# Expert sum and residual as diagonal matmuls in PSUM, last norm from PSUM, and SyncE waiting for the scatters itself

## The chip, the cores and the metric

The kernel runs on one core of a Trainium2 chip. The metric is the device time of one launch in microseconds (us), as the median of several runs. The core has five engines that run programs of their own and meet at semaphores: TensorE (PE, with its weight loads as PEld), VectorE (DVE), ScalarE (ACT), GpSimd (POOL) and SyncE (SP), which here only issues transfers. A smaller number is better.

## What is computed

One transformer layer on 512 tokens of width 1024: attention and a state space layer, a first layer norm, and then a mixture of 64 experts of which each token uses two. The change lies in the last two lines, where the two expert rows of a token are weighted and summed, the scaled residual is added, and the result is normalised.

```python
def layer_norm(x, g, b):
    mu = mean(x); var = mean((x - mu)**2)
    return (x - mu) * rsqrt(var + LN_EPS) * g + b

x = layer_norm(DN_ALPHA * x + mixed @ w_out, ln1_g, ln1_b)   # 512 x 1024, float32
# router: for every token two experts e0, e1 and two weights w0, w1
# y0 = expert_e0(x), y1 = expert_e1(x)       (silu(x @ w_gate) * (x @ w_up)) @ w_down
y_m = w0 * y0 + w1 * y1
x = layer_norm(DN_ALPHA * x + y_m, ln2_g, ln2_b)             # the output
```

## The kernel before

**Stages.** Projections, attention and the state space layer run first. Then comes the first norm, and after it the router. From the router's choices VectorE builds tables: which expert each block of 64 tokens uses (`ids`), which tokens are in it (`gidx`), and where its rows are written (`sidx`). The names `idf` and `ids` stand for one row of numbers on one partition; `ids[MAXB]` holds `extra`, how many blocks there are beyond the first eight (`FORCED`). After `ids` is written (semaphore `s_idr`), VectorE goes on in the same program to the tables that free the first gather (`s_slot`, `s_idx`).

**Expert stage.** Per block SP loads the expert's weights (3 MB, six slots), POOL gathers the tokens from DRAM (`x1_dram`), PE turns them, multiplies (`gate_up` at L725, `down` at L745), ACT copies the result out of PSUM (L952), and POOL scatters it by an indirect transfer to a DRAM buffer `ye_scratch` (L1554). Each engine has its own copy of the loop: 6 rounds of 12 steps, each step inside an `If` that is skipped once the step's number reaches `extra`. In this case 62 blocks run, so 54 of the 72 steps of the loop are taken and the last 18 are skipped.

**Tail.** The text below calls what follows the last block the tail. POOL, behind its loop, waits until all scatters (`s_sct`) and gathers have landed and raises `s_moe`. SP waits for it (L378) and issues four loads, one for each tile of 128 tokens: both expert rows of a token, 1 MB each, into `yt`. VectorE then does `combine(t)`: row 0 times its weight plus the residual `x1t` (L1461; ACT has multiplied the residual by `ALPHA` during the router, at L938), row 1 times its weight added (L1462), and the sums of the norm (`norm_stats`, L1283 to L1286). ACT takes the square root (L970) and, after two small VectorE operations (`scales2`, L1467 and L1468), forms the normalised tile (L974). VectorE multiplies by the gain (L1478), POOL adds the offset (L1584), and SP writes the tile out (L381). The order on VectorE is written by hand: the sum of tile j, the scales of tile j-1, the gain of tile j-2.

Matmuls are in float32; 512 columns fill one PSUM bank, `ps[0]` to `ps[7]`. `s_ye` says that ACT has emptied a result bank.

## Time and profile before

| | us |
|---|---|
| median of 3 runs | 1080.71 |
| lowest, highest | 1080.68, 1081.19 |
| the profiled execution's own time | 1079.19 |
| its span in the trace | 1077.4 |

All times of the trace are counted from the start of the span. A row of the chain of waits or of the timeline gives the start, the length and the instruction; "L1462" is line 1462 of the kernel. "Idle before" is what the engine waited for ahead of an instruction. PEclk is the granted clock of TensorE: 1.00 is 2.4 GHz and 0.50 is 1.2 GHz. In this trace each float32 matmul that is not a transpose shows as two records.

### The profile page before, as it was taken

The numbers are of one execution on the slowest core, as the hardware profiler recorded it, in microseconds if no ns is written. First come the engines' busy times: TensorE is split into PE (matmuls) and PEld (weight loads), VectorE is DVE, ScalarE is ACT, GpSimd is POOL, SyncE is SP. The second block draws the span as 40 slices with busy tenths as digits, with TensorE's granted clock in tenths as the row PEclk, the third lists the DMA queues.
The fourth block names the chain that finished last, engine by engine and source line by source line (L and its number), as shares of the span: only waits on it lengthen the run. The fifth ranks groups of instructions, "written<-read, shape, count | busy, mean of one in ns | idle before, by whom it ended". The sixth has DMA issues, their size and how long they took to land.

```text
span 1077.4 us, 14172 instructions
## 1 busy us (share of the span) xinstructions
PE 883.6 (82%) x4862; PEld 492.9 (46%) x4862; DVE 312.7 (29%) x769; ACT 182.1 (17%) x400; POOL 175.6 (16%) x271
## 2 busy tenths in 40 slices
PE   7999887989999999998458888888888777788800
PEld 3446774544444444345435555555544344444400
DVE  5970744760111111144431111111111111111145
ACT  1223136661000100000201111111111010110111
POOL 2010002440000000000012222222222222222203
PEclk9999978999999999999569999999999999999955
DMA  8332903018222110532429999999999999999241
GB/s 285 72 87 69 116 22 142 1 69 351 113 100 99 69 69 0 203 133 112 161 78 411 420 421 420 421 421 422 422 421 422 421 424 424 424 424 408 91 158 78
DMA packets 43307, 253.36 MB, mean 235 GB/s; under 512 B 15304, under 2 KB 15832, under 8 KB 25956
## 3 DMA queue, kind: packets, MB, share of 16 engines
q1 hardware_dynamic: 32596, 242.58, 57.2%
q0 software_dynamic: 10528, 9.72, 3.5%
q8 instruction: 24, 0.39, 0.2%
q10 hardware_dynamic: 144, 0.55, 0.1%
q14 instruction: 15, 0.11, 0.0%
HBM read 256.27 MB, written 21.04 MB: 257 GB/s over the span
## 4 chain that ended last, share of the span: by engine, by line
PE 59%; DMA 17%; SPq 8%; DVE 6%; issue 4%; ACT 4%; POOLq 0%; POOL 0%; DVEq 0%; ACTq 0%
PE ps L623 18%; DMA arena<-experts 11%; PE ps L725 11%; PE ps L745 6%; PE ps L398 5%; PE ps L660 5%; SPq L330 4%; DMA reg_a<-experts 4%; PE ps L390 3%; SPq L307 2%; ACT arena L883 2%; PE ps L590 2%; PE ps L714 2%; SPq L327 1%; PE ps L544 1%
## 5 line engine op out<-in xcount | busy, mean ns | idle before, releaser
L725 PE MATMUL ps<-arena,xT 128*64 128x256 f32 x1344 | 155.2, 383 | 19.8 <-DMA arena<-experts 18.4
L725 PEld LDWEIGHTS ps<-arena,xT 128*64 128x64 f32 x1344 | 106.9, 138 | 81.5 <-issue 49.4
L1430 DVE TENSOR_TENSOR reg_bo<-reg_bo,ps 128x128 f32<-128x128 f32 x62 | 17.8, 287 | 364.6 <-ACT reg_bo L945 364.6
L623 PE MATMUL ps<-xT,arena 128*128 128x512 f32 x256 | 111.7, 594 | 2.1 <-PE ps L623 2.1
L1554 POOL DMA_INDIRECT ye_scratch<-xT,reg_u x62 | 62.2, 1003 | 253.8 <-ACT xT L952 253.8
L745 PE MATMUL ps<-arena,reg_bo 128*64 128x512 f32 x336 | 81.4, 601 | 18.2 <-issue 17.2
L623 PEld LDWEIGHTS ps<-xT,arena 128*128 128x128 f32 x256 | 48.1, 190 | 65.6 <-issue 65.6
L952 ACT COPY xT<-ps 128x512 f32<-128x512 f32 x62 | 36.3, 585 | 202.6 <-PE ps L745 202.6
L945 ACT ACTIVATE reg_bo<-ps 128x128 f32<-128x128 f32 x62 | 17.2, 277 | 239.7 <-PE ps L725 239.7
L623 PE MATMUL ps<-reg_u,arena 128*128 128x512 f32 x128 | 57.5, 592 | 0.0
L660 PE MATMUL ps<-reg_a,reg_bo 128*128 128x512 f32 x128 | 55.5, 593 | 2.3 <-DVE reg_bo L1276 2.3
L398 PE MATMUL ps<-xT,reg_bo 128*128 128x512 f32 x128 | 55.7, 594 | 0.0
L1543 POOL DMA_INDIRECT reg_a<-x_scratch,reg_u x34 | 36.1, 1062 | 105.1 <-PE ps L714 103.2
L1270 DVE TENSOR_TENSOR arena<-arena,ps 128x512 f32<-128x512 f32 x8 | 5.5, 687 | 158.2 <-PE ps L623 158.2
L919 ACT ACTIVATE arena<-ps,small 128x512 f32<-128x512 f32 x24 | 16.5, 687 | 171.5 <-PE ps L623 171.5
L745 PEld LDWEIGHTS ps<-arena,reg_bo 128*64 128x64 f32 x336 | 24.0, 136 | 46.6 <-issue 46.6
L1527 POOL MEMSET reg_a<- 128x1024 f32 x2 | 1.8, 949 | 265.3 <-PE ps L660 265.3
L1422 DVE COPY xT<-ps 128x512 f32<-128x512 f32 x64 | 41.2, 685 | 7.8 <-PE ps L714 7.8
L714 PE MATMUL ps<-small,reg_a 128*128 128x128 f32 x256 | 35.8, 284 | 6.9 <-DMA reg_a<-x_scratch,reg_u 6.9
L735 PE MATMUL ps<-small,reg_bo 128*128 128x128 f32 x62 | 20.1, 324 | 26.0 <-DVE reg_bo L1430 26.0
L725 PE MATMUL ps<-reg_bo,xT 128*64 128x256 f32 x320 | 36.6, 381 | 3.8 <-DMA reg_bo<-experts 3.8
L1519 POOL TENSOR_SCALAR arena<-arena,reg_a 128x512 f32<-128x512 f32 (+2 forms) x48 | 30.8, 653 | 50.9 <-DVE arena L1229 50.9
(249 smaller groups left out, 1048.5 us busy)
## 6 DMA issues: line engine op xcount, KB each, us to landing
arena<-experts SPq DMA_DIRECT2D x42, 2048.0 KB, 36.3
arena<-experts SPq DMA_DIRECT2D x42, 1024.0 KB, 35.7
reg_bo<-experts SPq DMA_DIRECT2D x10, 2048.0 KB, 37.3
reg_a<-experts SPq DMA_DIRECT2D x10, 2048.0 KB, 37.9
arena<-mid_w SPq DMA_DIRECT2D x8, 1792.0 KB, 7.4
reg_bo<-experts SPq DMA_DIRECT2D x10, 1024.0 KB, 36.5
reg_a<-experts SPq DMA_DIRECT2D x10, 1024.0 KB, 37.3
reg_bo<-front_w SPq DMA_DIRECT2D x12, 512.0 KB, 3.3
```

The source lines that it names most:

```text
L330: sp_.dma_start(slots[k][:, GU:EW], a["experts"][rows, GU:EW]).then_inc(s_wd[k], 16)
L390: m = pe.matmul(ps[k // 2][64 * (k % 2):64 * (k % 2) + 64, :], xTc[:, c, k:L:T8], w_u[:, c, :], start=(c == 0), stop=(c == KC - 1))
L398: m = pe.matmul(ps[bank][:, :], ring[:, i % 4, c * P:(c + 1) * P], xTc[:, c, :], start=(c == 0), stop=(c == KC - 1))
L623: m = pe.matmul(ps[bank][:, :], w[:, (o + c) * P:(o + c + 1) * P], rhs[:, c, :], start=(c == 0), stop=(c == nk - 1))
L660: m = pe.matmul(ps[2 * t + h][:, :], mixT[:, c, t * P:(t + 1) * P], w_out[:, c, h * 512:(h + 1) * 512], start=(c == 0), stop=(c == KC - 1))
L714: m = pe.transpose(ps[c // 4][:, (c % 4) * P:(c % 4 + 1) * P], xg[q][:, c * P:(c + 1) * P], eye)
L725: m = pe.matmul(ps[2 + c % 2][64 * h:64 * h + 64, 0:DE], xgT[q][:, x, BLK * (c % 2):BLK * (c % 2 + 1)], slots[k][:, x * 512 + h * DE:x * 5 ...
L745: m = pe.matmul(ps[6 + c % 2][64 * j:64 * j + 64, :], hT[c % 2][:, 64 * h:64 * h + 64], slots[k][:, GU + h * D + j * 512:GU + h * D + (j + ...
L952: act.copy(yb[c % 4], ps[6 + c % 2][:, :]).then_inc(s_ye, 1)
L1422: c = dve.tensor_copy(xgT[q][:, 4 * h:4 * h + 4, :], ps[h][:, :].rearrange("p (c t) -> p c t", c=4))
L1543: pool.indirect_dma_start(xg[q], None, x1_dram, bass.IndirectOffsetOnAxis(gcol[q], 0), bounds_check=L - 1, oob_is_err=False).then_inc(s_g[ ...
L1554: pool.indirect_dma_start(ye_dram, bass.IndirectOffsetOnAxis(scol[k], 0), yb[k], None, bounds_check=4 * L - 1, oob_is_err=False).then_inc( ...
```

## The change

**Sum on TensorE.** VectorE forms eight diagonal matrices behind its loop, one for each tile and each of the two expert rows, with the tokens' weights on the diagonal, and a ninth with `ALPHA` (`diags`, `alpha_eye`; semaphore `s_diag`). PE, behind its loop, multiplies them with the residual (`residual(t)`, two matmuls) and with the loaded rows (`expert_rows(t)`, four matmuls), all into two PSUM banks per tile, and raises `s_sum`. The residual is no longer scaled by ACT.

**Norm on VectorE.** `finish(t)` takes the sums of the norm from PSUM, forms (x - mean) * gain from PSUM into `yt[:, t, 0]`, and then times 1/std plus offset into `yt[:, t, 1]`. ACT keeps the square roots alone, and POOL has nothing left in the tail but its waits.

**SyncE waits itself.** VectorE writes four more numbers into `ids`, the final values of the four scatter semaphores; SP reads them and waits for `s_sct` directly in place of `s_moe`.

```diff
+        diags = [wdiag[:, n, :] for n in range(7)] + [ediag[:, 0, :]]
+        alpha_eye = ediag[:, 1, :]
 # SyncE
-            sp_.wait_ge(s_moe, 1)
+            written = [sp_.value_load(ids[0:1, MAXB + 2 + j:MAXB + 3 + j], min_val=16, max_val=4 * MAXB) for j in range(4)]
+            for j in range(4):
+                sp_.wait_ge(s_sct[j], written[j])
...
-                sp_.dma_start(a["out"][t * P:(t + 1) * P, :], yt[:, t, 0, :]).then_inc(s_out, 16)
+                sp_.dma_start(a["out"][t * P:(t + 1) * P, :], yt[:, t, 1, :]).then_inc(s_out, 16)
 # TensorE
+            def residual(t):
+                for h in range(2):
+                    pe.matmul(ps[2 * t + h][:, :], alpha_eye, x1t[:, t, h * 512:(h + 1) * 512], start=True, stop=False)
+            def expert_rows(t):
+                pe.wait_ge(s_yt[t], 16)
+                for k in range(2):
+                    for h in range(2):
+                        m = pe.matmul(ps[2 * t + h][:, :], diags[TT * k + t], yt[:, t, k, h * 512:(h + 1) * 512],
+                                      start=False, stop=(k == 1))
+                m.then_inc(s_sum, 1)
+            pe.wait_ge(s_diag, 1)
+            pe.wait_ge(s_ye, extra + FORCED)
+            residual(0)
+            residual(1)
+            for t in range(TT):
+                expert_rows(t)
+                if t + 2 < TT:
+                    residual(t + 2)
 # ScalarE
-            act.mul(x1t, x1t, ALPHA).then_inc(s_xs, 1)
...
-                    act.activation(yt[:, t, 1, :], yt[:, t, 0, :], ACT.Identity, bias=lnst[:, 52 + t:53 + t],
-                                   scale=lnst[:, 36 + t:37 + t]).then_inc(s_hat, 1)
 # VectorE, router
-            dve.tensor_scalar(ids[0:1, MAXB + 1:MAXB + 2], ids[0:1, MAXB + 1:MAXB + 2], 3, None, ALU.bitwise_and).then_inc(s_idr, 1)
+            put(dve.tensor_scalar(ids[0:1, MAXB + 1:MAXB + 2], ids[0:1, MAXB + 1:MAXB + 2], 3, None, ALU.bitwise_and))
+            for j in range(4):
+                put(dve.tensor_scalar(ids[0:1, MAXB + 2 + j:MAXB + 3 + j], idf[:, MAXB:MAXB + 1], float(FORCED + 3 - j), None, ALU.add))
+            dve.wait_ge(s_dve, n_dve[0])
+            link(dve.tensor_scalar(ids[0:1, MAXB + 2:MAXB + 6], ids[0:1, MAXB + 2:MAXB + 6], 252, None, ALU.bitwise_and))
+            dve.tensor_scalar(ids[0:1, MAXB + 2:MAXB + 6], ids[0:1, MAXB + 2:MAXB + 6], 2, None, ALU.logical_shift_left).then_inc(s_idr, 1)
 # VectorE, tail
+            for k in range(2):
+                for t in range(TT):
+                    dve.tensor_scalar(diags[TT * k + t], eye, wts[:, k, t:t + 1], None, ALU.mult)
+            dve.tensor_scalar(alpha_eye, eye, ALPHA, None, ALU.mult).then_inc(s_diag, 1)
             dve.wait_ge(s_row2, 32)
...
+            def finish(t):
+                dve.wait_ge(s_sum, t + 1)
+                for h in range(2):
+                    put(dve.bn_stats(lnst[:, 40 + 6 * h:46 + 6 * h], ps[2 * t + h][:, :]))
+                dve.wait_ge(s_dve, n_dve[0])
+                link(dve.bn_aggr(lnst[:, 8 * t:8 * t + 2], lnst[:, 40:52]))
+                dve.tensor_scalar(lnst[:, 8 * t + 1:8 * t + 2], lnst[:, 8 * t + 1:8 * t + 2], EPS, None, ALU.add).then_inc(s_var, 1)
+                for h in range(2):
+                    put(dve.scalar_tensor_tensor(yt[:, t, 0, h * 512:(h + 1) * 512], ps[2 * t + h][:, :], lnst[:, 8 * t:8 * t + 1],
+                                                 ln2g[:, h * 512:(h + 1) * 512], ALU.subtract, ALU.mult))
                 dve.wait_ge(s_std, TT + t + 1)
+                put(dve.reciprocal(lnst[:, 36 + t:37 + t], lnst[:, 32 + t:33 + t]))
+                dve.wait_ge(s_dve, n_dve[0])
+                dve.scalar_tensor_tensor(yt[:, t, 1, :], yt[:, t, 0, :], lnst[:, 36 + t:37 + t], ln2b, ALU.mult, ALU.add).then_inc(s_ln2, 1)
 # GpSimd
-            pool.nop().then_inc(s_moe, 1)
-            pool.wait_ge(s_row2, 32)
-            for t in range(TT):
-                pool.wait_ge(s_gain, t + 1)
-                pool.tensor_tensor(yt[:, t, 0, :], yt[:, t, 1, :], ln2b, ALU.add).then_inc(s_ln2, 1)
```

The program of TensorE ended with the loop's last step. These are its last rows before; L735 and L745 are the last step's transpose and its `down`.

```order
L735 MATMUL ps5<-small,reg_bo 128x128 [waits s_he,s_h]
L745 MATMUL ps7<-arena,reg_bo 64x512 [waits s_ye,s_he,s_wd1]
L745 MATMUL ps7<-arena,reg_bo 64x512 x3
L769 UNCONDITIONAL_BRANCH
L767 REGISTER_ALU
L767 COMPARE_AND_BRANCH
L66 UNCONDITIONAL_BRANCH
```

These are its last rows after the change; L780 is `residual`, L786 is `expert_rows`, and `reg_u` holds the diagonal matrices.

```order
L786 MATMUL ps3<-arena,reg_u 128x512
L780 MATMUL ps6<-x1,reg_u 128x512
L780 MATMUL ps7<-x1,reg_u 128x512
L786 MATMUL ps4<-arena,reg_u 128x512 [waits s_yt2]
L786 MATMUL ps5<-arena,reg_u 128x512
L786 MATMUL ps4<-arena,reg_u 128x512
L786 MATMUL ps5<-arena,reg_u 128x512
L786 MATMUL ps6<-arena,reg_u 128x512 [waits s_yt3]
L786 MATMUL ps7<-arena,reg_u 128x512
L786 MATMUL ps6<-arena,reg_u 128x512
L786 MATMUL ps7<-arena,reg_u 128x512
L66 UNCONDITIONAL_BRANCH
```

The residual of tile 3 stands between the rows of tiles 1 and 2, and each tile has two banks of its own.

On VectorE these rows stood for one tile in the middle of the tail before (tile 3, with the gain of tile 1 ahead of it).

```order
L1478 TENSOR_TENSOR arena<-arena,reg_u 128x1024 [waits s_hat]
L1461 SCALAR_TENSOR_TENSOR arena<-arena,reg_u,x1 128x1024 [waits s_yt3]
L1462 SCALAR_TENSOR_TENSOR arena<-arena,reg_u 128x1024 [waits s_dve]
L1283 BN_STATS reg_u<-arena 128x6 [waits s_dve]
L1283 BN_STATS reg_u<-arena 128x6
L1285 BN_AGGR reg_u<-reg_u 128x2 [waits s_dve]
L1286 TENSOR_SCALAR reg_u<-reg_u 128x1 [waits s_dve]
L1467 RECIPROCAL reg_u<-reg_u 128x1 [waits s_std]
L1468 SCALAR_TENSOR_TENSOR reg_u<-reg_u 128x1 [waits s_dve]
```

And these stand for tile 3 after the change.

```order
L1487 BN_STATS reg_u<-ps6 128x6 [waits s_sum]
L1487 BN_STATS reg_u<-ps7 128x6
L1489 BN_AGGR reg_u<-reg_u 128x2 [waits s_dve]
L1490 TENSOR_SCALAR reg_u<-reg_u 128x1 [waits s_dve]
L1492 SCALAR_TENSOR_TENSOR arena<-ps6,reg_u 128x512
L1492 SCALAR_TENSOR_TENSOR arena<-ps7,reg_u 128x512
L1495 RECIPROCAL reg_u<-reg_u 128x1 [waits s_std]
L1497 SCALAR_TENSOR_TENSOR arena<-arena,reg_u 128x1024 [waits s_dve]
```

The two long sums and the gain are gone, and two reads of PSUM and one long operation on SBUF take their place.

In the router, VectorE's rows at `ids` were these before.

```order
L1379 CAST reg_u<-reg_u 1x1
L1380 TENSOR_SCALAR reg_u<-reg_u 1x1
L1381 TENSOR_SCALAR reg_u<-reg_u 1x1 [waits s_dve]
L992 TENSOR_TENSOR reg_u<-ps3,reg_u 128x256
L1385 TENSOR_REDUCE reg_u<-reg_u 128x4 [waits s_dve]
```

After the change they are these.

```order
L1397 CAST reg_u<-reg_u 1x1
L1398 TENSOR_SCALAR reg_u<-reg_u 1x1
L1399 TENSOR_SCALAR reg_u<-reg_u 1x1 [waits s_dve]
L1401 TENSOR_SCALAR reg_u<-reg_u 1x1 x4
L1403 TENSOR_SCALAR reg_u<-reg_u 1x4 [waits s_dve]
L1404 TENSOR_SCALAR reg_u<-reg_u 1x4 [waits s_dve]
```

Six small instructions and two waits for VectorE's own results are added ahead of the tables of the gather.

## Rows read from the trace of the kernel before

**Rows 1.** The page: the span.

```profile
span 1077.4 us, 14172 instructions
```

**Rows 2.** The chain of waits, 1015 to 1078 us: start, length, what.

```profile
976.97 39.29 DMA arena<-experts
...
1023.84 0.59 ACT xT L952
...
1025.27 0.04 POOL ye_scratch L1554
...
1031.03 5.43 DMA arena<-ye_scratch
```

**Rows 3.** The DMA queue's own waits, SyncE, 960 to 1078 us.

```profile
SPq L378 <- POOLq L1580: 42.8, 1, 42.8
...
SPq L66 <- PEq L66: 6.3, 1, 6.3
SPq L66 <- DMA out<-arena: 2.3, 1, 2.3
```

**Rows 4.** Line L1554, the last scatter alone (1020 to 1030 us): issue to landing.

```profile
DMA to landing us min/median/max: 2.3/2.3/2.3
```

**Rows 5.** Line L378, the four loads of the expert rows: issue to landing.

```profile
DMA to landing us min/median/max: 5.4/8.6/11.6
```

**Rows 6.** The timeline, 1012 to 1078 us: start, length, instruction, idle before it.

```profile
1021.38 0.29 DVE L1437 COPY reg_bo<-ps 128x128 f32<-128x128 f32 x1 [0.42 <-PE ps L735]
...
1028.11 1.28 ACT L970 ACT_TABLE_LOAD   x1 [3.69 <-issue]
...
1039.23 1.29 DVE L1283 BATCH_NORM_STATS2 reg_u<-arena 128x6 f32<-128x512 f32 x2
...
1040.80 0.15 DVE L1286 TENSOR_SCALAR reg_u<-reg_u 128x1 f32<-128x1 f32 x1
1040.87 1.27 DVE L1461 SCALAR_TENSOR_TENSOR arena<-arena,reg_u,x 128x1024 f32<-128x1024 f32 x1
...
1052.38 3.25 DVE L1462 SCALAR_TENSOR_TENSOR arena<-arena,reg_u 128x1024 f32<-128x1024 f32 x1
...
1065.93 2.34 POOL L1584 TENSOR_TENSOR arena<-arena,reg_u 128x1024 f32<-128x1024 f32 x1 [1.16 <-DVE arena L1478]
```

**Rows 7.** Groups by line and shape, whole span: busy us, mean ns of one.

```profile
L660 PE MATMUL ps<-reg_a,reg_bo 128*128 128x512 f32 x128 | 55.5, 593 | 2.3 <-DVE reg_bo L1276 2.3
...
L1305 DVE SCALAR_TENSOR_TENSOR x<-x,ps 128x512 f32<-128x512 f32 x8 | 5.1, 680 | 20.9 <-PE ps L660 20.9
...
L992 DVE TENSOR_TENSOR x<-arena 128x128 f32<-128x128 f32 x4 | 0.9, 286 | 0.0
```

**Rows 8.** Busy time of each engine by stretch; PEclk stands after POOL.

```profile
1027.50:1028.00 0.50, 0.00 (x0) 0.00 (x0) 0.00 (x0) 0.00 (x0) 0.00 (x0) 0.62 0.00 0
1028.00:1077.40 49.40, 0.00 (x0) 0.00 (x0) 28.39 (x36) 7.05 (x9) 10.25 (x4) 0.50 0.32 128
...
557.10:559.50 2.40, 2.34 (x12) 1.59 (x14) 0.00 (x0) 0.00 (x0) 0.64 (x2) 0.50 0.17 38
...
560.00:562.30 2.30, 2.30 (x21) 1.42 (x19) 0.00 (x0) 0.05 (x1) 0.00 (x0) 1.00 0.00 0
```

**Rows 9.** The timeline of TensorE, 504 to 562 us: L676 at either clock, first `gate_up`.

```profile
506.76 2.02 PE L676 MATMUL ps<-reg_u,xT 128*128 128x96 f32 x16 [1.16 <-ACT xT L930]
...
514.57 3.73 PE L676 MATMUL ps<-reg_u,xT 128*128 128x96 f32 x16 [1.16 <-ACT xT L930]
...
557.16 5.05 PE L725 MATMUL ps<-arena,xT 128*64 128x256 f32 x32 [1.47 <-DVE xT L1422]
```

**Rows 10.** The timeline of the router, 518 to 558 us, at `ids`.

```profile
535.69 0.13 DVE L1380 TENSOR_SCALAR reg_u<-reg_u 1x1 uint32<-1x1 f32 x1
535.85 0.14 DVE L1381 TENSOR_SCALAR reg_u<-reg_u 1x1 uint32<-1x1 uint32 x1
535.92 0.40 DVE L992 TENSOR_TENSOR reg_u<-ps,reg_u 128x256 f32<-128x256 f32 x1
```

More of the change, by code:

```diff
@@ L227, in build_kernel @@
         ln2g, ln2b = reg_u[:, 0:D], reg_u[:, 1315:1315 + D]
+        wdiag = reg_u[:, 1315 + D:1315 + D + 7 * P].rearrange("p (n m) -> p n m", n=7)
+        ediag = reg_u[:, D:D + 2 * P].rearrange("p (n m) -> p n m", n=2)
+        diags = [wdiag[:, n, :] for n in range(7)] + [ediag[:, 0, :]]
+        alpha_eye = ediag[:, 1, :]
         yt = arena[:, 0:8192].rearrange("p (t k n) -> p t k n", t=TT, k=2)
@@ L260, in build_kernel @@
         s_nb = sem("s_nb"); s_st = sem("s_st"); s_base = sem("s_base"); s_ids = sem("s_ids")
-        s_slot = sem("s_slot"); s_tbl = sem("s_tbl"); s_xs = sem("s_xs")
+        s_slot = sem("s_slot"); s_tbl = sem("s_tbl")
         s_idx = sem("s_idx"); s_idr = sem("s_idr"); s_x1d = sem("s_x1d")
@@ L266, in build_kernel @@
         s_xt = sem("s_xt"); s_xe = sem("s_xe"); s_gu = sem("s_gu"); s_silu = sem("s_silu"); s_h = sem("s_h")
-        s_ht = sem("s_ht"); s_he = sem("s_he"); s_dn = sem("s_dn"); s_ye = sem("s_ye"); s_moe = sem("s_moe")
+        s_ht = sem("s_ht"); s_he = sem("s_he"); s_dn = sem("s_dn"); s_ye = sem("s_ye"); s_diag = sem("s_diag"); s_sum = sem("s_sum")
         s_yt = [sem(f"s_yt{t}") for t in range(TT)]; s_ln2 = sem("s_ln2")
-        s_row2 = sem("s_row2"); s_out = sem("s_out"); s_nrm = sem("s_nrm"); s_hat = sem("s_hat"); s_gain = sem("s_gain")
+        s_row2 = sem("s_row2"); s_out = sem("s_out")
         STAGE = ((3,), (2,), (0, 1))
@@ L935, in _ @@
             act.activation(r4[1][:, 0, :], r4[1][:, 0, :], ACT.Exp).then_inc(s_ge, 1)
-            act.wait_ge(s_x1d, 16 * TT)
-            act.wait_ge(s_xt1, TT)
-            act.mul(x1t, x1t, ALPHA).then_inc(s_xs, 1)
             def silu(i, c):
@@ L965, in _ @@
                         step(i, FORCED + j)
-            for j in range(TT + 1):
-                if j < TT:
-                    act.wait_ge(s_var, TT + j + 1)
-                    act.activation(lnst[:, 32 + j:33 + j], lnst[:, 8 * j + 1:8 * j + 2], ACT.Sqrt).then_inc(s_std, 1)
-                if j >= 1:
-                    t = j - 1
-                    act.wait_ge(s_nrm, t + 1)
-                    act.activation(yt[:, t, 1, :], yt[:, t, 0, :], ACT.Identity, bias=lnst[:, 52 + t:53 + t],
-                                   scale=lnst[:, 36 + t:37 + t]).then_inc(s_hat, 1)
+            for t in range(TT):
+                act.wait_ge(s_var, TT + t + 1)
+                act.activation(lnst[:, 32 + t:33 + t], lnst[:, 8 * t + 1:8 * t + 2], ACT.Sqrt).then_inc(s_std, 1)
         @block.vector
@@ L1453, in _ @@
                         step(i, FORCED + j)
+            for k in range(2):
+                for t in range(TT):
+                    dve.tensor_scalar(diags[TT * k + t], eye, wts[:, k, t:t + 1], None, ALU.mult)
+            dve.tensor_scalar(alpha_eye, eye, ALPHA, None, ALU.mult).then_inc(s_diag, 1)
             dve.wait_ge(s_row2, 32)
-            dve.wait_ge(s_xs, 1)
-            def combine(t):
-                y0, y1 = yt[:, t, 0, :], yt[:, t, 1, :]
-                dve.wait_ge(s_yt[t], 16)
-                link(dve.scalar_tensor_tensor(y0, y0, wts[:, 0, t:t + 1], x1t[:, t, :], ALU.mult, ALU.add))
-                link(dve.scalar_tensor_tensor(y0, y1, wts[:, 1, t:t + 1], y0, ALU.mult, ALU.add))
-                norm_stats(t, y0, s_var)
@@ L1465, in scales2 @@
-            def scales2(t):
-                dve.wait_ge(s_std, TT + t + 1)
-                link(dve.reciprocal(lnst[:, 36 + t:37 + t], lnst[:, 32 + t:33 + t]))
-                dve.scalar_tensor_tensor(lnst[:, 52 + t:53 + t], lnst[:, 8 * t:8 * t + 1], -1.0, lnst[:, 36 + t:37 + t],
-                                         ALU.mult, ALU.mult).then_inc(s_nrm, 1)
-            for j in range(TT + 2):
-                if j < TT:
-                    combine(j)
-                if 1 <= j <= TT:
-                    scales2(j - 1)
-                if j >= 2:
-                    dve.wait_ge(s_hat, j - 1)
-                    dve.tensor_tensor(yt[:, j - 2, 1, :], yt[:, j - 2, 1, :], ln2g, ALU.mult).then_inc(s_gain, 1)
+            def finish(t):
[8 more added lines that the diff above has]
+                                                 ln2g[:, h * 512:(h + 1) * 512], ALU.subtract, ALU.mult))
+                dve.wait_ge(s_std, TT + t + 1)
+                put(dve.reciprocal(lnst[:, 36 + t:37 + t], lnst[:, 32 + t:33 + t]))
+                dve.wait_ge(s_dve, n_dve[0])
+                dve.scalar_tensor_tensor(yt[:, t, 1, :], yt[:, t, 0, :], lnst[:, 36 + t:37 + t], ln2b, ALU.mult, ALU.add).then_inc(s_ln2, 1)
@@ L1481, in _ @@
+            for t in range(TT):
+                finish(t)
         @block.gpsimd
```

## The prediction

> **What bounds the kernel now.** I read the chain of waits first, at its end. The last expert's weights land at 1016.3 us, the last block passes PE and ACT until 1024.4, and POOL starts the last scatter at 1025.27 [rows 2]. Nothing of the change touches the expert stage ahead of that. What follows is the tail, and there the chain is a single line: the scatter, the wait of SP, the first load of expert rows (1031.03, 5.43 us long), then VectorE without a gap, and POOL's last add, which ends at 1065.93 + 2.34 = 1068.27 [rows 2, 6]. So the tail from the scatter's start is 43.0 us, and what lies between the last add and the end of the span is 1077.4 - 1068.3 = 9.1 us [rows 1]: the last write (2.3) and a wait at the end of the program (6.3) [rows 3], which the change leaves alone. The reader should see two things in the tail. First, SP stood ready for 42.8 us and was released by POOL's L1580, not by a transfer [rows 3]. Second, VectorE needs about 4.27 us for a tile before the gains begin (1036.60 to 1040.87 [rows 2, 6]), and then its long operations grow from 1.28 to 3.25 us while POOL adds beside it [rows 6].
>
> **The change part by part.** All sums are made in the time of the profiled execution.
>
> *SP waits itself.* The last scatter is issued at 1025.27 and lands 2.3 us later, at 1027.6 [rows 2, 4]. SP issued the first load at 1031.03 only because POOL first had to pass the 18 skipped steps of its loop: ACT's idle time of 3.69 us for its own 18, with nothing to wait for, gives their price, 0.2 us each [rows 6]. SP has passed its own skipped steps, and will have read its four numbers, long before, under the 42.8 us for which it waits [rows 3]; without that cover the reads would cost a microsecond or two. The gain is 1031.0 - 1027.6 = **3.4 us**. It can't be more, since the rows must have landed. At least it is 0, if the landing is seen late. I take 3.4.
>
> *The loads.* Unchanged: 5.43 us to the first landing [rows 2], so 1033.0. The fourth lands 11.6 us after its own issue at the longest [rows 5], about 1041; PE asks for it at 1047 (below). Hidden.
>
> *Diagonals and first residuals.* VectorE ends its last block at 1021.67, and 18 skipped steps bring it to 1025.4 [rows 6]. Then nine operations of 128x128. The nearest rows took 0.9 us for four, 0.22 each [rows 7]: 2.0 us, to 1027.4. PE itself ends its last matmul at 1023.7 and its skipped steps at about 1027.4. So `residual(0)` and `residual(1)`, four matmuls, start at about 1027.6. One matmul is two records, and 128 records of the same shape took 55.5 us [rows 7]: **0.434 us a record, 0.867 us a matmul**, at 2.4 GHz. Four are 3.5 us. But in this very place the clock falls: PEclk is 0.62 between 1027.5 and 1028.0 and 0.50 from there on, after 4 us without a matmul [rows 8]. What 1.2 GHz costs is shown by L676, whose 16 records took 2.02 us at the one clock and 3.73 at the other [rows 9]; I take a factor of 2 for 512 columns. Four cold matmuls take 6.9 us, to 1034.5. The clock rose at 560.0 in the first `gate_up`, 2.8 us after it began, with PE busy all the way [rows 8, 9]. [...] Bounds: nothing, or 1.5 us of delay. I take nothing.
>
> *Expert rows on PE.* 4 matmuls a tile are 3.47 us, and with the residual of a later tile 5.2 us. From 1033.0: the first tile's sum stands at 1036.7 (the last record's tail is 0.16), tile 1 at 1041.9, tile 2 at 1047.1, tile 3, which has no residual behind tile 2, at 1050.5.
>
> *VectorE's `finish(t)`.* Two sums of the norm to the aggregate's start, 1.33 us; aggregate 0.24; the add, behind which the next operation starts after 0.07 [rows 6]; two operations of 512 columns from PSUM at 0.6 a start, 0.68 long [rows 7], 1.2; the reciprocal and the wait for the operation ahead, 0.2; 128x1024 on SBUF, 1.3 [rows 6]. Sum **4.4 us**. This is below PE's 5.2, so tiles 0 to 2 follow PE: tile 2 runs from 1047.1 to 1051.5, tile 3 from there to **1055.9**. ACT's square root (0.2 us) lies beside the two PSUM operations. The whole of L1461, L1462, L1478, ACT's L974 and POOL's L1584 is gone from the end, and with POOL silent nothing stretches VectorE. Against 1068.27 this is **12.4 us** less, of which 3.4 is SP's and 9.0 the shorter work. No row shows the sums of the norm from PSUM; bounds are 4.1 and 5.0 us for `finish`, of which only two stand on the path, so -0.6 to +1.2 us. The Trainium skill ("VectorE: DVE Perf Modes", the section on the errata) speaks against reading PSUM: its table gives a fixed 120 cycles for a PSUM source against 58 for SBUF. By it, estimated, four such operations a tile would add 0.26 us, 0.5 us on the path. The rows say otherwise: 512 columns took 680 ns with PSUM [rows 7], and two sums of the norm on SBUF 1.29 us together, which at 0.6 a start leaves 0.69 for one [rows 6].
>
> *The four numbers in the router.* One instruction that depends on the one ahead starts 0.16 to 0.2 us after it, one that doesn't 0.07 [rows 10]. Added are four of the second kind (0.28), a wait for them (0.14), and one of the first kind (0.2): **+0.6 us**. Nothing covers it: VectorE alone works there, the gather waits for its tables, and the expert stage starts later by as much. The first `gate_up` took 5.05 us because the clock rose within it [rows 9]; shifted, it may meet the rise 0.3 us better or lose up to 2.2 us if the rise comes after its end (all at 1.2 GHz, 2 x 3.63 us). I take 0.6, bounds 0.3 and 2.8.
>
> *ACT's scaling of the residual* (L938) is off. It ran beside VectorE's router work and nobody in the expert stage waited for it: nothing.
>
> **Sum.** -12.4 + 0.6 = -11.8 us. The profiled execution (1079.19) lies 1.5 us under the median of 1080.71; the difference is put on the median: **1068.9 us**.
>
> **The rivals.**
>
> *A: the sum holds.* 1068.9.
>
> *B: the clock comes up a stage late.* PE may reach `expert_rows(0)` with the clock still at 1.2 GHz, or lose it in the gap ahead of the rows. For it speaks that L676 ran at 0.50 for 3.7 us without a rise [rows 9]. Against it, that the new matmuls leave no gap. Residuals to 1034.5 (+1.5) and the first tile cold (+3.5): 5.0 us, 1073.9.
>
> *C: the clock stays down.* The one mechanism by which this becomes slower: TensorE has not a single matmul in the tail today, and its clock is at 0.50 for the last 49 us [rows 8]. With 1.73 us a matmul, the 20 matmuls from the landing on end at 1034.5 + 34.7 = 1069.2, and `finish(3)` at 1073.6, 5.3 us after POOL's end of before; with the router's 0.6 it is +5.9, **1086.6 us**. It turns slower from about 1.5 us a matmul on ((1067.7 - 4.4 - 1033.0) / 20), so only if most of the stretch runs at 1.2 GHz. Against it stands the rise at 560.0 [rows 8].
>
> *D: the change doesn't bring SP forward.* If the last scatter's semaphores reach SP no sooner than they released POOL, the 3.4 us stay, and PE, idle after the residuals, may drop its clock once more for part of tile 0 (1 us or so): 1072.3 to 1073.5. For it: POOL shows no wait for a transfer, so the trace can't tell when the semaphores were full, but by the landing, and 2.3 us is the figure against [rows 4]. The Trainium skill ("DMA: Bandwidth & Descriptors", the anatomy of one DMA) says that the completion of a write to HBM can take long. By that rule, the 2.3 us already hold it, so the trace agrees with its 2.0 us.
>
> **How the numbers follow.** A 0.70, B 0.12, C 0.05, D 0.08, and 0.05 for a gain larger than A's by more than a microsecond. The range should leave out C and the far end of the gain, and hold B and D: 1066.8 (A with `finish` at its lower bound, the router at 0.3, and half a microsecond of difference between runs) to 1074.0. About 0.2% (2.2 us) is what a measurement of this kernel can tell from no change. B and D are faster too. Faster 0.93, same 0.02, slower 0.05.
>
> **What would show it.** SP's first load at about 1028.2 (1027.6 and the router's 0.6), released by a transfer and not by POOL. The first sum 3.6 us behind the first landing. VectorE idle for about 0.8 us ahead of tiles 1 and 2 and not ahead of tile 3, each `finish` at 4.4 us. The last operation of `finish(3)` (L1497 of the changed kernel) ends at 1056.5, and the span at 1065.6. The granted clock at 0.50 in the first residuals and at 1.00 from the first rows on. The first gather 0.6 us later. What would make it wrong: a PE record of 512 columns at 0.85 us in the tail, a `finish` of more than 5.2 us, so that VectorE sets the pace, or an end of the program longer than 9.1 us now that PE works in it.

## The result: 1064.1 us, 16.7 us less than before

| | before | changed kernel |
|---|---|---|
| median of the runs | 1080.78 us (1080.68 to 1081.19, 4 runs) | 1064.13 us (1062.71 to 1067.44, 4 runs) |
| ratio | | 0.985, 95% interval 0.9825 to 0.9875 |
| profiled execution, its span | 1079.19, 1077.4 us | 1063.05, 1061.3 us |
| mean granted clock of TensorE | 0.944 | 0.961 |

The change gained 16.65 us. I had predicted 11.8 (1068.9 us, at best 1066.8), so the time lies below the range of 1066.8 to 1074.0, in the direction to which the prediction had given a chance of 0.05. The page of the changed kernel, its span and two rows of its slices: PE now works to the end, and its clock is up there.

```profile
span 1061.3 us, 14282 instructions
...
PE   7999977989999999999529888888887787777866
...
PEclk9999978999999999999659999999999999999999
```

Three stretches account for the two spans. The last scatter of expert rows starts at 1026.70 instead of 1025.27 (+1.43). From there to the end of the last operation it takes 1058.21 - 1026.70 = 31.5 us instead of 43.0 (-11.5). From that end to the end of the span it takes 3.1 us instead of 9.1 (-6.0). The sum is -16.1, the difference of the spans. The prediction had +0.6, -12.4 and 0.

**The tail.** This is the timeline of the changed kernel from 1022 us on (start, length, engine, line and operation, idle time before it and what ended that); it answers to [rows 6].

```profile
1026.70 0.98 POOL L1576 DMA_INDIRECT ye_scratch<-xT,reg_u  x1 [6.72 <-ACT xT L976]
1028.23 1.66 DVE L1480 TENSOR_SCALAR reg_u<-small,reg_u 128x128 f32<-128x128 f32 x8 [5.12 <-issue]
1029.05 2.41 SPq L384 DMA_DIRECT2D arena<-ye_scratch  x4
...
1030.57 5.08 PE L780 MATMUL ps<-x,reg_u 128*128 128x512 f32 x8 [5.42 <-DVE reg_u L1481]
...
1035.49 3.60 PE L786 MATMUL ps<-arena,reg_u 128*128 128x512 f32 x8
...
1039.19 1.30 DVE L1487 BATCH_NORM_STATS2 reg_u<-ps 128x6 f32<-128x512 f32 x2 [9.17 <-PE ps L786]
...
1044.27 1.30 DVE L1487 BATCH_NORM_STATS2 reg_u<-ps 128x6 f32<-128x512 f32 x2 [0.65 <-PE ps L786]
...
1049.42 1.30 DVE L1487 BATCH_NORM_STATS2 reg_u<-ps 128x6 f32<-128x512 f32 x2 [0.71 <-PE ps L786]
...
1051.07 1.40 DVE L1492 SCALAR_TENSOR_TENSOR arena<-ps,reg_u 128x512 f32<-128x512 f32 x2
...
1053.78 1.29 DVE L1487 BATCH_NORM_STATS2 reg_u<-ps 128x6 f32<-128x512 f32 x2
...
1056.92 1.29 DVE L1497 SCALAR_TENSOR_TENSOR arena<-arena,reg_u 128x1024 f32<-128x1024 f32 x1
```

These rows show the chain that the prediction described: scatter, first load 2.35 us later, four residual matmuls (8 records), then the expert rows, and VectorE idle for 0.65 and 0.71 us ahead of tiles 1 and 2 and not at all ahead of tile 3. The last two tiles are 1053.78 - 1049.42 = 4.36 us apart.

**The end.** The DMA queue's own waits from 955 us on, which answer to [rows 3]: time in total, how often, the longest.

```profile
SPq L381 <- DMA ye_scratch<-xT,reg_u: 37.0, 2, 19.7
...
SPq L66 <- DMA out<-arena: 2.3, 1, 2.3
...
SPq L66 <- PEq L66: 0.2, 1, 0.2
```

SyncE is released by the scatters and no longer by GpSimd. The wait for the last write is the 2.3 us of before. The wait named PEq, 6.3 us before [rows 3], is 0.2. Those are the 6 us that I had not forecast. L66 is where every engine ends the program. In its records an engine has a DRAIN there and then the semaphores at which all engines meet. These are the DRAINs of VectorE and GpSimd before, and that of GpSimd after the change (durations in ns, then the start):

```profile
L66 DVEq DRAIN  x1: 3361/3361/3361, 1062.5 to 1062.5; - x1
L66 POOLq DRAIN  x1: 11296/11296/11296, 1065.9 to 1065.9; - x1
```

```profile
L66 POOLq DRAIN  x1: 8894/8894/8894, 1032.4 to 1032.4; - x1
```

Before, GpSimd's DRAIN is recorded from 1065.9 to 1077.2, the end of the span. It holds the last add, which ends at 1068.27, and then another 8.9 us. In the changed kernel GpSimd has nothing to do after the scatters. Its DRAIN takes the same 8.9 us, but begins at 1032.4 and is over at 1041.3, beside everyone else's work.

### The profile page after: what moved, and what is told of

It reads as the page before. It is cut to its first block, busy times and chain, and to the rows that moved or that the text cites. A ratio compares the mean times of both kernels' runs of the same rounds, so it can differ in the third digit from the quotient of the medians.

```text
span 1061.3 us, 14282 instructions
## 1 busy us (share of the span) xinstructions
PE 905.8 (85%) x4910; PEld 502.7 (47%) x4910; DVE 303.9 (29%) x780; ACT 173.7 (16%) x395; POOL 165.6 (16%) x267
## 4 chain that ended last, share of the span: by engine, by line
PE 62%; DMA 16%; SPq 8%; DVE 5%; ACT 4%; issue 4%; DVEq 0%; ACTq 0%; POOL 0%; POOLq 0%
PE ps L629 18%; PE ps L731 11%; DMA arena<-experts 11%; PE ps L751 6%; PE ps L404 5%; PE ps L666 5%; SPq L334 4%; DMA reg_a<-experts 4%; PE ps L396 3%; SPq L311 2%; ACT arena L910 2%; PE ps L596 2%; PE ps L720 2%; SPq L331 1%; PE ps L786 1%
## 5 line engine op out<-in xcount | busy, mean ns | idle before, releaser
L666 PE MATMUL ps<-reg_a,reg_bo 128*128 128x512 f32 x128 | 55.5, 593 | 2.3 <-DVE reg_bo L1294 2.3
L666 PEld LDWEIGHTS ps<-reg_a,reg_bo 128*128 128x128 f32 x128 | 24.1, 190 | 32.3 <-issue 32.3
```

Source lines behind the costliest of these rows:

```text
L666: m = pe.matmul(ps[2 * t + h][:, :], mixT[:, c, t * P:(t + 1) * P], w_out[:, c, h * 512:(h + 1) * 512], start=(c == 0), stop=(c == KC - 1))
```

## The experiments

Two theories of the 6 us were tested by experiment. **G**: GpSimd's DRAIN takes 8.9 us, and the others wait for it. (G1: counted from the point at which GpSimd reaches it; G2: counted from GpSimd's last operation.) **T**: it is TensorE's work in the tail that shortens the end. (A third, that the end varies by itself, is out: it takes 3.0 to 3.1 us in nine of the profiled executions and 9.1 to 9.4 in the four in which GpSimd has something at the end.) The further runs take the terms of the sum one by one. All times within a batch were taken beside runs of the kernel before; their medians were 1080.83, 1081.24 and 1081.71 us.

| kernel | batch | median (range), us | ratio, 95% | first load after scatter | scatter to last operation | last operation to end |
|---|---|---|---|---|---|---|
| before | | 1080.78 | 1 | 5.76 | 43.0 | 9.1 |
| changed | | 1064.13 | 0.985 | 2.35 | 31.5 | 3.1 |
| e1: add on VectorE, nothing else | 1 | 1071.63 (1069.5 to 1072.11) | 0.9885 to 0.9939 | 5.76 | 39.3 | 3.1 |
| e2: changed, GpSimd waits | 1 | 1069.18 (1067.15 to 1071.96) | 0.9865 to 0.9929 | 2.36 | 33.0 | 9.4 |
| e3: and writes | 1 | 1071.84 (1070.33 to 1072.08) | 0.9891 to 0.9944 | 2.35 | 32.9 | 9.3 |
| e4: SyncE's part undone | 1 | 1064.52 (1062.01 to 1066.24) | 0.9822 to 0.9884 | 5.76 | 34.2 | 3.1 |
| e5: sum on VectorE | 2 | 1066.68 (1065.6 to 1069.94) | 0.9845 to 0.9875 | 2.35 | 35.7 | 3.1 |
| e6: residuals after the rows | 2 | 1070.24 (1068.51 to 1070.85) | 0.9876 to 0.9906 | 2.35 | 36.9 | 3.1 |
| e7: diagonals early | 2 | 1066.08 (1063.13 to 1066.95) | 0.9835 to 0.9864 | 2.35 | 33.0 | 3.1 |
| e8: changed, again | 2 | 1064.42 (1063.53 to 1066.33) | 0.9829 to 0.9857 | 2.35 | 33.0 | 3.0 |
| e9: rows of tile 1 first | 3 | 1063.58 (1062.37 to 1066.18) | 0.9808 to 0.9859 | 2.36 | 32.2 | 3.0 |
| e10: offset on GpSimd again | 3 | 1071.08 (1069.73 to 1073.64) | 0.9879 to 0.9942 | 2.35 | 33.1 | 9.2 |
| e11: changed, third time | 3 | 1064.45 (1061.11 to 1066.58) | 0.9826 to 0.9877 | 2.35 | 31.5 | 3.0 |

The last three columns are read from the profiled executions, by start and length of the named instructions; in e3 the last operation is VectorE's. From the first load of the expert loop to the last scatter all thirteen executions took 463.0 to 463.3 us, so no difference in the table comes from there. The last three columns belong to the tail alone; the medians also hold what varies ahead of the expert loop (last section).

### e1: the kernel before, with GpSimd's add on VectorE

```
-                    dve.tensor_tensor(yt[:, j - 2, 1, :], yt[:, j - 2, 1, :], ln2g, ALU.mult).then_inc(s_gain, 1)
+                    link(dve.tensor_tensor(yt[:, j - 2, 1, :], yt[:, j - 2, 1, :], ln2g, ALU.mult))
+                    dve.tensor_tensor(yt[:, j - 2, 0, :], yt[:, j - 2, 1, :], ln2b, ALU.add).then_inc(s_ln2, 1)
...
-                pool.wait_ge(s_gain, t + 1)
-                pool.tensor_tensor(yt[:, t, 0, :], yt[:, t, 1, :], ln2b, ALU.add).then_inc(s_ln2, 1)
```

> The kernel before, with one edit: the offset of the last norm (L1584) is added by VectorE and not by GpSimd; sum, scales and waits stay. The prediction took the 9.1 us between the last add and the end of the span as fixed. Theory G (GpSimd's end): GpSimd's last instruction at the end of the program, a DRAIN, takes about 8.9 us from the end of its last work and all engines wait for it; with the add gone it ends under the tail, and the end of the program falls from 6.3 us of waiting for an engine to under 0.5 us. Work: VectorE gets 4 x 1.22 us more and loses the stretching beside GpSimd, so the last add ends 2 to 3 us sooner. Together 8 to 9 us faster, about 1072. Theory T (TensorE's end): the 6.3 us fell away because TensorE works in the tail of the changed kernel; then they stay here, since TensorE has no work in this tail, and only the 2 to 3 us come, about 1078. Theory F (the end varies by itself): no fixed difference.

Measured: 9.2 us less than before, more than half of the whole change, by moving four additions. The end is 3.1 us, with TensorE as idle in the tail as before. The queue's own waits and the record of GpSimd's end:

```profile
SPq L66 <- DMA out<-arena: 2.3, 1, 2.3
...
SPq L66 <- PEq L66: 0.2, 1, 0.2
```

```profile
L66 POOLq DRAIN  x1: 8894/8894/8894, 1033.8 to 1033.8; - x1
```

T has fallen: there is no matmul in this tail. The other 3.7 us (43.0 to 39.3, where 2 to 3 were expected) are a balance. VectorE's 128x1024 operations take 1.22 to 1.28 us everywhere in this tail. Before, three of its operations were longer beside GpSimd's adds: the 3.25 us of [rows 6], the one below, and a 128x1 operation (L1468, at 1058.89) that took 2.32 us and not 0.16.

```profile
1062.52 3.32 DVE L1478 TENSOR_TENSOR arena<-arena,reg_u 128x1024 f32<-128x1024 f32 x1 [0.17 <-ACT arena L974]
```

Together that is 6.2 us, and GpSimd's last add another 2.4 with its handover. Against them stand four adds on VectorE, some 5.0 us, which leaves 3.6.

### e2 and e3: the changed kernel, GpSimd waits for the last tile, and in e3 also writes one column

```
                         pool.wait_ge(s_g[q], 4 * n - 4 * k + 32 + 16 * (q == 0 and k >= 2))
+            pool.wait_ge(s_ln2, TT)
+            pool.memset(reg_a[:, 0:1], 0.0)
```

(e2 has the first added line alone.)

> The changed kernel, with GpSimd waiting for the last tile (s_ln2) behind its loop before it ends; it computes nothing there. Theory G1 (the DRAIN costs 8.9 us whenever it is reached): it starts at the end of the last tile and ends 8.9 us later, the program ends 5.8 us later than the changed kernel's, about 1070. Theory G2 (the 8.9 us count from GpSimd's last real operation): the DRAIN is short and the time is the changed kernel's, about 1064. Theory T: no change either.

> As the run before, and behind the wait GpSimd sets one column of 128 numbers. Theories G1 and G2 both expect the 5.8 us back, about 1070: the DRAIN ends 8.9 us after this small operation. Theory T expects no change, about 1064. Together with the run before it tells whether the wait or the operation starts the 8.9 us.

Measured, e2, the end's records and the wait:

```profile
L66 POOLq DRAIN  x1: 8897/8897/8897, 1058.7 to 1058.7; - x1
```

```profile
SPq L66 <- PEq L66: 6.5, 1, 6.5
```

And e3:

```profile
L66 POOLq DRAIN  x1: 9019/9019/9019, 1060.6 to 1060.6; - x1
```

```profile
SPq L66 <- PEq L66: 6.4, 1, 6.4
```

The end is 9.4 us in e2 and 9.3 in e3. The median of e3 is 2.7 us above that of e2, but their tails are alike (33.0 and 32.9 us); in e3's profiled execution the tail began 2.2 us later. A bare wait, with no operation behind it and no work added to any engine, brings the 6 us back. That is G1. G2 would have left e2 at 3.1. The name PEq in the wait is therefore misleading: of several that SyncE waited for at L66, GpSimd was the last. With e1 (6 us go with GpSimd's work alone) and e2 (they come back with GpSimd's wait alone) this cause is shown from both sides. What the 8.9 us consist of, no run tells.

### e10: the changed kernel, the offset added on GpSimd again

```
-                dve.scalar_tensor_tensor(yt[:, t, 1, :], yt[:, t, 0, :], lnst[:, 36 + t:37 + t], ln2b, ALU.mult, ALU.add).then_inc(s_ln2, 1)
+                dve.tensor_scalar(yt[:, t, 1, :], yt[:, t, 0, :], lnst[:, 36 + t:37 + t], None, ALU.mult).then_inc(s_gain, 1)
...
+                pool.wait_ge(s_gain, t + 1)
+                pool.tensor_tensor(yt[:, t, 1, :], yt[:, t, 1, :], ln2b, ALU.add).then_inc(s_ln2, 1)
```

> The changed kernel, with one part of it undone: the offset of the norm is added by GpSimd again, behind a VectorE multiplication by 1/std. Theory G: GpSimd's DRAIN starts behind the last add and takes 8.9 us, so the end of the program grows from 3.1 to 9.1 us; and the last add itself lies on the path, 2.3 us, where VectorE's last operation gets 0.5 us shorter. Together 7.5 to 9 us slower than the changed kernel, about 1072.5. Rival (the add costs only itself): 2 us slower, about 1066.5.

Measured: 6.6 us more than the changed kernel in the same batch. The timeline at the end and the end's record:

```profile
1056.82 0.75 DVE L1497 TENSOR_SCALAR arena<-arena,reg_u 128x1024 f32<-128x1024 f32 x1
1057.65 2.34 POOL L1605 TENSOR_TENSOR arena<-arena,reg_u 128x1024 f32<-128x1024 f32 x1 [1.47 <-DVE arena L1497]
```

```profile
L66 POOLq DRAIN  x1: 11296/11296/11296, 1057.6 to 1057.6; - x1
```

Each VectorE operation ahead of an add is 0.53 us shorter, the add takes 2.34, and the end is 9.2 us again. The recorded 11296 ns are those of before to the nanosecond: 2.34 of the add and 8.96 behind it. The tail to the last operation is 1.6 us longer than the changed kernel's, 0.2 of it in the residuals (5.26 to 5.08). So the add costs the path 1.4 us as an operation, and 6.1 more because it makes GpSimd finish late. By the trace that is 7.5 us, at the lower bound of the expectation, and by the medians 6.6, below it; the rival's 2 us is out.

### e4: SyncE's part undone

```
...
-            for j in range(4):
-                sp_.wait_ge(s_sct[j], written[j])
+            sp_.wait_ge(s_moe, 1)
...
+            pool.nop().then_inc(s_moe, 1)
```

The router's four added numbers and their loads on SyncE are gone with it.

> The changed kernel with SyncE's part undone: SyncE waits for GpSimd's s_moe again, and the four numbers in the router are left out. My account: the first load starts 5.8 us after the last scatter's start and not 2.35, the first gate_up starts 0.5 us sooner. TensorE ends its first two residuals either way, and idles up to 3 us ahead of the rows, in which its clock may fall again. Expected 3.4 - 0.7 (the residuals no longer delay the first rows) - 0.5 = 2.2 us slower than the changed kernel, up to 4 us if the clock falls. Rival (the load's start doesn't matter since the residuals and their cold clock set the first rows): within 0.7 us of the changed kernel.

The timeline has the effect as predicted:

```profile
1030.38 2.81 SPq L382 DMA_DIRECT2D arena<-ye_scratch  x4
...
1036.01 3.70 PE L784 MATMUL ps<-arena,reg_u 128*128 128x512 f32 x8 [2.38 <-DMA arena<-ye_scratch]
```

The first load is issued 5.76 us after the scatter instead of 2.35, TensorE waits 2.38 us for the rows, and the tail is 2.7 us longer than in the changed kernel (34.2 to 31.5). But the medians, 1064.52 and 1064.13, don't tell them apart: in its profiled execution the tail began 2.1 us earlier, of which the router's missing instructions explain 0.6. So the 2.7 us are read in the tail, and in the time of the whole kernel this run is inconclusive.

### e5: the changed kernel, the weighted sum on VectorE again

```
+                link(dve.scalar_tensor_tensor(y0, y0, wts[:, 0, t:t + 1], x1t[:, t, :], ALU.mult, ALU.add))
+                link(dve.scalar_tensor_tensor(y0, y1, wts[:, 1, t:t + 1], y0, ALU.mult, ALU.add))
                 for h in range(2):
...
+                    put(dve.bn_stats(lnst[:, 40 + 6 * h:46 + 6 * h], yt[:, t, 0, h * 512:(h + 1) * 512]))
...
```

The diagonals and TensorE's matmuls in the tail are gone, ACT scales the residual as before, and the norm keeps its new order, on SBUF.

> The changed kernel with the sum moved back: VectorE forms the weighted sum and adds the residual (scaled by ScalarE during the router) as before, TensorE has nothing in the tail; the new norm without ScalarE's and GpSimd's share, SyncE's direct wait and the short end stay. A tile costs VectorE 2.6 + 4.4 = 7.0 us from SBUF. My account: first landing 7.8 us after the last scatter's start, then 4 x 7.0, so 35.8 us to the last operation's end against 31.5 to 33 in the changed kernel: 3 to 4 us slower than it, about 1067.5, so TensorE's part is worth only 3 to 4 of the 16.6 us. Rival (TensorE's sum is what brought the end of the program forward): 9 to 10 us slower, about 1074.

```profile
1044.47 1.28 DVE L1467 SCALAR_TENSOR_TENSOR arena<-arena,reg_u,x 128x1024 f32<-128x1024 f32 x1
...
1051.33 1.28 DVE L1467 SCALAR_TENSOR_TENSOR arena<-arena,reg_u,x 128x1024 f32<-128x1024 f32 x1
```

A tile now takes VectorE 6.86 us (1051.33 - 1044.47), the first one starts as soon as its rows are there, and the tail is 35.7 us. TensorE's sum is worth 35.7 less 31.5 to 33.0, 2.7 to 4.2 us, by when the clock rises in the changed kernel (e8 below). By the medians of the batch it is 2.3 us, with intervals that just overlap. It is the most elaborate part of the change and not its largest.

### e6: the first residuals wait for the rows

```
             pe.wait_ge(s_ye, extra + FORCED)
+            pe.wait_ge(s_yt[0], 16)
             residual(0)
```

> The changed kernel, with the first residual matmul waiting for the first rows to land. My account: TensorE then begins cold at the landing (7.8 us after the scatter's start), 4 residual and 4 row matmuls stand ahead of the first sum, of which the first 3 to 6 us run at 1.2 GHz: first rows 5 to 6.6 us after the landing, against 0.8 to 2.5 in the changed kernel, so 4 to 5 us slower. Rival (the clock does not rise in this tail unless matmuls ran ahead): all 20 at 1.73 us, over 15 us slower.

```profile
1037.40 6.08 PE L780 MATMUL ps<-x,reg_u 128*128 128x512 f32 x8 [9.85 <-DMA arena<-ye_scratch]
1043.32 3.60 PE L786 MATMUL ps<-arena,reg_u 128*128 128x512 f32 x8
```

Even after 9.85 us without a matmul the clock rises within the residuals: the expert rows run at 0.43 us a record (8 in 3.60). From landing to first rows it takes 6.1 us (1043.32 less 1031.46 + 5.8), where it takes 0.7 in the changed kernel and 2.3 in e8 (1038.76 less 1030.87 + 5.6). So doing the residuals under the loads gains 3.8 to 5.3 us, and the tails agree (36.9 us against 33.0 and 31.5, expected were 4 to 5). The medians of the batch differ by 5.8 us; the 1.9 us beyond the 3.9 between its tail and e8's are not in the tail. Rival C, a clock that stays down, has no support in any run.

### e7 and e8: the diagonals built at the start of the expert stage, and the control

```
             for c in range(FORCED):
                 step(0, c)
+            for k in range(2):
+                for t in range(TT):
+                    dve.tensor_scalar(diags[TT * k + t], eye, wts[:, k, t:t + 1], None, ALU.mult)
+            dve.tensor_scalar(alpha_eye, eye, ALPHA, None, ALU.mult).then_inc(s_diag, 1)
             dve.wait_ge(s_idr, 1)
```

> The changed kernel, with VectorE forming the nine diagonal matrices behind its eighth block and not behind its loop. In the changed kernel the first residual started 3.9 us after the last scatter's start, since VectorE's 18 skipped steps took 5.1 us and the diagonals 1.8; the rows then waited 0.8 to 2.5 us for TensorE. My account: the residuals start at about 2.2 us, held by TensorE's own skipped steps, and the first rows start 0 to 1 us after the landing: 0.8 to 1.5 us faster than the changed kernel of the same batch. Rival (TensorE's own loop or the clock holds them): within 0.3 us.

> The changed kernel again, beside the others. From the last scatter's start to the last operation's end 31.5 us, or up to 33 where the clock comes up later in the residuals; the end of the program 3.1 us. The time from the first expert load of the loop to the last scatter is 463 us in every kernel; what differs between runs, by 3 us or so, lies ahead of that load. About 1064.

e7's residuals:

```profile
1033.06 6.52 PE L780 MATMUL ps<-x,reg_u 128*128 128x512 f32 x8 [5.42 <-issue]
```

e8's:

```profile
1032.42 6.50 PE L780 MATMUL ps<-x,reg_u 128*128 128x512 f32 x8 [5.46 <-DVE reg_u L1481]
```

I had taken VectorE's diagonals for what held the first residual. The wait for them is gone in e7, and yet TensorE starts 3.87 us after the scatter, within 0.03 us of e8 (3.90) and the changed kernel (3.87). The idle 5.42 us end by themselves, at the end of TensorE's own 18 skipped steps. My account fell and the rival held: the tail is 33.0 us in both, and the edit gains nothing. (The median is 1.7 us above e8's, more than the rival's 0.3, with intervals that overlap almost wholly; no row of the tail accounts for it.)

The control shows something else. Its residuals took 6.50 us where the changed kernel's took 5.08, and that is the whole difference of their tails (33.0 and 31.5). The granted clock in the changed kernel, by stretch (length; PE, PEld, DVE, ACT, POOL busy; clock, DMA share, GB/s), which answers to [rows 8]:

```profile
1029.50:1030.00 0.50, 0.00 (x0) 0.00 (x0) 0.50 (x3) 0.46 (x1) 0.00 (x0) 0.98 0.00 0
1030.00:1030.50 0.50, 0.00 (x0) 0.00 (x0) 0.02 (x1) 0.50 (x1) 0.00 (x0) 0.50 0.57 131
1030.50:1033.00 2.50, 2.43 (x3) 1.18 (x4) 0.00 (x0) 0.33 (x1) 0.00 (x0) 0.50 0.98 347
...
1033.50:1034.00 0.50, 0.50 (x2) 0.22 (x2) 0.00 (x0) 0.00 (x0) 0.00 (x0) 1.00 0.99 410
```

and in e8:

```profile
1036.00:1037.00 1.00, 1.00 (x3) 0.48 (x2) 0.00 (x0) 0.00 (x0) 0.00 (x0) 0.50 1.01 418
1037.00:1056.00 19.00, 19.00 (x44) 8.12 (x42) 11.87 (x24) 0.61 (x3) 0.00 (x0) 0.97 0.45 183
```

In the changed kernel TensorE had been idle since 1025.2 when the clock fell to 0.50 (1.2 GHz) at 1030.0. It rose to 1.00 some 2.8 us after the first residual in the one execution (at 1033.4), and 5.7 us after it in the other (at about 1038.1). The same program meets the rise early (the residuals take 5.08 us in the changed kernel and 5.09 in e11) or late (6.50 in e8). So do the kernels that differ from it elsewhere: early in e4 and e10 (5.15, 5.26), late in e2, e3, e7 and e9 (6.57, 6.42, 6.52, 6.66). Rival B came true in part, in its 1.5 us for the residuals, and without its cold first tile.

### e9 and e11: the rows of tile 1 ahead of the residual of tile 2, and the control

```
-            for t in range(TT):
+            expert_rows(0)
+            expert_rows(1)
+            for t in range(2, TT):
+                residual(t)
                 expert_rows(t)
-                if t + 2 < TT:
-                    residual(t + 2)
```

> The changed kernel, with TensorE taking the rows of tile 1 right behind those of tile 0 and the residuals of tiles 2 and 3 just ahead of their own rows. My account, from the start of the first row matmul: the sums of tiles 0 to 3 stand at 3.6, 7.1, 12.3 and 17.5 us (before: 3.6, 8.8, 13.9, 17.4), VectorE with 4.36 us a tile sets the pace for tiles 1 and 2, and the last operation ends at 21.9 and not at 22.7: 0.8 us faster than the changed kernel of the same batch, a little over what five rounds can tell. The idle time of VectorE ahead of its second and third tile goes, one of 0.8 us ahead of the fourth comes. Rival (VectorE slows down while TensorE writes other banks): within 0.2 us.

> The changed kernel once more, beside the two runs above. 31.5 to 33 us from the last scatter's start to the last operation's end, 3.1 us for the end of the program, about 1064. If the spread of a few us between runs comes from TensorE's clock ahead of the expert stage, as the profiles so far point to, the time from the first expert load of the loop to the last scatter stays 463 us here too, and the start of the first gate_up lies anywhere between 555 and 561 us.

```profile
1039.56 7.03 PE L786 MATMUL ps<-arena,reg_u 128*128 128x512 f32 x16
...
1047.62 1.29 DVE L1488 BATCH_NORM_STATS2 reg_u<-ps 128x6 f32<-128x512 f32 x2
...
1056.93 1.29 DVE L1488 BATCH_NORM_STATS2 reg_u<-ps 128x6 f32<-128x512 f32 x2 [0.53 <-PE ps L786]
...
1060.08 1.28 DVE L1498 SCALAR_TENSOR_TENSOR arena<-arena,reg_u 128x1024 f32<-128x1024 f32 x1
```

VectorE no longer waits ahead of tiles 1 and 2 and waits 0.53 us ahead of tile 3. From the first matmul of expert rows to the last operation it takes 61.36 - 39.56 = 21.8 us, in the changed kernel and e8 22.7: 0.9 us less. The medians, 1063.58 and 1064.45, have intervals that overlap almost wholly. By the trace of the tail this order is the better one; by the time it is not told apart. e11, the control, answers its question only in part: the loop took 463 us and the first `gate_up` began at 555.86, both as expected, but its lead over the changed kernel (1061.11 us against 1063.05) comes from a wait for a transfer and not from the clock (last section).

## Why the prediction was wrong, point by point

**The step that failed** is in the first paragraph of the prediction: it took the 9.1 us between the last add and the end of the span, "the last write (2.3) and a wait at the end of the program (6.3)", as something "which the change leaves alone", and gave no reason. The row of that wait named TensorE's queue [rows 3], which misled. The wait was the end of GpSimd's part, 8.9 us behind its last instruction. The change takes GpSimd's last instruction away from the end, and what is left is the 2.3 us of the write. That is 6.0 us, more than the whole miss of 4.8 (1068.9 less 1064.13). With an end of 9.1 us the change would have come to some 1070.1 us, 1.2 above the prediction and inside its range. The prediction even named the end as what could make it wrong, but only in the other direction. The record of GpSimd's end was in the trace of before, 11.3 us long and ending with the span.

**SyncE waits itself: right.** First load 2.35 us after the scatter's start (2.3 predicted), released by the transfers. Rival D is out. Its four reads (L379) ran from 989.7 to 991.9, long before the scatter. In e4, which undoes this part alone, the tail is 2.7 us longer.

**The loads: 0.3 us longer.** Landing of the four, by the line that issues them, which answers to [rows 5]:

```profile
DMA to landing us min/median/max: 5.7/8.8/11.8
```

**First residuals: 1.6 us late, and the first rows 1.1.** I had 18 skipped steps at ACT's price, 3.7 us. VectorE's took 5.12 and TensorE's 5.42 (ACT's 3.69 again). So the residuals start 3.87 us after the scatter instead of 2.3 and end 0.7 us after the landing (1035.49 to 1029.05 + 5.7), where I had taken no delay. No row or run shows that term to be nothing, and it is not a constant: in e8, where the clock rises later, the rows wait 2.3 us for the residuals. With the loads' 0.3 the first sum stands 12.5 us after the scatter instead of 11.4.

**The clock: right.** 0.50 in the first residuals and 1.00 from the first rows on, as forecast from [rows 8, 9]. In e8 the clock rises just ahead of the rows, and e6 has it too, after 9.85 us without a matmul. A record of expert rows starts every 0.43 us, and a tile of rows and residual is 5.15 us (1035.49, 1040.64, 1045.79) against 5.2.

**`finish`: right.** 4.36 us against 4.4. VectorE's pauses are 0.65 and 0.71 us against 0.8 (5.2 less 4.4). Two sums of the norm from PSUM took 1.30 us, where they took 1.29 from SBUF [rows 6]. By the fixed cost of a PSUM source that the Trainium skill states ("VectorE: DVE Perf Modes", the errata) they would have taken, estimated, some 0.13 us more. This trace doesn't show that cost for the pair of sums (0.01 us of difference).

**The router: right, and what came behind it a term too small.** The rows at `ids`, which answer to [rows 10], and the first `gate_up` [rows 9]:

```profile
535.68 0.14 DVE L1399 TENSOR_SCALAR reg_u<-reg_u 1x1 uint32<-1x1 uint32 x1
535.75 0.31 DVE L1401 TENSOR_SCALAR reg_u<-reg_u 1x1 uint32<-1x1 f32 x4
536.10 0.16 DVE L1403 TENSOR_SCALAR reg_u<-reg_u 1x4 uint32<-1x4 uint32 x1
536.29 0.16 DVE L1404 TENSOR_SCALAR reg_u<-reg_u 1x4 uint32<-1x4 uint32 x1
536.37 0.41 DVE L1010 TENSOR_TENSOR reg_u<-ps,reg_u 128x256 f32<-128x256 f32 x1
...
557.69 5.96 PE L731 MATMUL ps<-arena,xT 128*64 128x256 f32 x32 [1.47 <-DVE xT L1445]
```

From L1399 to L1010 there are 0.69 us, 0.07 before: 0.62 against 0.6. `gate_up` starts 0.53 us later and takes 5.96 instead of 5.05, because the clock rises at about 562.4 instead of 560.0. So the expert stage is 1.4 us late where I had taken 0.6 (bounds 0.3 and 2.8). In the other kernels `gate_up` took 5.5 to 6.4 us, e1 (5.89), whose router is that of before, among them. So the 0.9 us go with the moment at which the clock rises and not with the router's added work.

**The sum** of these, leaving the end aside, is +1.4 - 11.5 = -10.1 against -11.8. The forecast's mechanism held, with 1.7 us lost in small terms (the clock in `gate_up`, the loads, the residuals), and then 6.0 us came from outside of it. The lower bound of the range was also added up wrongly: the three allowances that it names, 0.6, 0.3 and 0.5 us, lead from 1068.9 to 1067.5 and not to 1066.8. The measured time lies below both.

**The parts of the gain**, in the tail from scatter to end of span: 52.1 us before. VectorE alone (e1) takes 9.7, 3.7 of stretching and waiting and 6.0 of GpSimd's end. SyncE's wait and the norm's new order (e5) take 3.6. TensorE's sum takes 2.7 to 4.2. The changed kernel is at 34.6 to 36.0. Its runs are spread over some microseconds by what differs between executions ahead of the tail (last section).

## What to carry to other kernels

Before the end of a program is entered as a constant, read the last instructions of every engine on its closing line, and ask which engine reaches it last, before and after the change. An engine whose own end takes long has to finish first, and here that was worth more than the arithmetic that the change moved. Where an engine passes skipped steps on the way to new work, take their time from that engine's own rows and not from another's.
